# A hybrid encoder layer: DeltaNet's gate projection as filling of the chunks, and another order of the last merge

## The reference

```
h = rmsnorm(x);  parts = split(h @ w_in)                       # nq, nk, nv, nz, nba belong to DeltaNet
y_gdn = rmsnorm(o_f + o_b, norm_g) * silu(nz)                  # o_f, o_b: chunked delta rule, both ways
merged = sum_i sigmoid(h @ merge_w[i] + merge_b[i]) * (y_i @ branch_up[i])      # i = 3 is DeltaNet
x = x + merged @ mix_out
x = x + cross_attention(rmsnorm(x), rmsnorm(mem))
x = x + moe(rmsnorm(x));  return rmsnorm(x)                    # 32 experts, two per token
```

## Time and profile before

| | us |
|---|---|
| Median of three executions | 2064.29 |
| The profiled execution, its own time | 2065.67 |
| Its span in the profile | 2063.9 |
| TensorE busy | 1909.5 (93%) |
| VectorE busy | 1388.5 (67%) |
| ScalarE busy | 1083.7 (53%) |
| TensorE in the chain that ended last | 79% of the span |

### The profile page before, as it was taken

How to read it: one execution, slowest core, us unless ns; L and a number is a source line. 1 busy time by engine, 2 the same in 40 slices (tenths; PEclk the granted TensorE clock), 3 DMA queues, 4 the chain that set the end, 5 groups by cost and what they waited for, 6 DMA issues and landing times.

```text
span 2063.9 us, 33015 instructions
## 1 busy us (share of the span) xinstructions
PE 1909.5 (93%) x13076; PEld 1138.2 (55%) x13076; DVE 1388.5 (67%) x1831; ACT 1083.7 (53%) x1582; POOL 324.1 (16%) x285
## 2 busy tenths in 40 slices
PE   6999999999999999999999999895899999999991
PEld 3464565655544545767488855685355444444440
DVE  4555533799865687634643845437799999999986
ACT  4563223666656432223333534334588888888862
POOL 6000100344300523421000000000001111111102
PEclk9999999999999999999999999997899999999995
DMA  5411111212011352332321500403799999999976
GB/s 185 161 51 42 32 42 53 66 47 57 24 39 47 118 179 83 113 108 99 138 67 48 168 32 21 167 31 152 268 423 422 422 422 421 422 422 422 422 290 261
DMA packets 140522, 360.45 MB, mean 175 GB/s; under 512 B 38224, under 2 KB 91632, under 8 KB 113776
## 3 DMA queue, kind: packets, MB, share of 16 engines
q1 hardware_dynamic: 96608, 279.57, 35.7%
q10 hardware_dynamic: 34944, 46.14, 6.4%
q0 software_dynamic: 8848, 33.03, 4.1%
HBM read 307.85 MB, written 46.66 MB: 172 GB/s over the span
## 4 chain that ended last, share of the span: by engine, by line
PE 79%; DVE 9%; ACT 5%; issue 4%; DMA 1%; SPq 1%; DVEq 0%; ACTq 0%; POOL 0%; POOLq 0%
PE psum L787 40%; PE psum L1194 24%; ACT arena L1636 2%; PE psum L1183 1%; PE psum L1118 1%; PE psum L1093 1%; DVE arena L2288 1%; PE psum L917 1%; PE psum L1212 1%; PE psum L804 1%; PE psum L1053 1%; PE psum L989 1%; DMA arena<-in_w_in_dram 1%; PE psum L979 1%; PE psum L928 1%
## 5 line engine op out<-in xcount | busy, mean ns | idle before, releaser
L787 PE MATMUL psum<-arena 128*128 128x512 f16 (+2 forms) x6000 | 1016.6, 327 | 7.7 <-issue 2.8
L787 PEld LDWEIGHTS psum<-arena 128*128 128x128 f16 x6000 | 569.6, 98 | 391.5 <-issue 23.5
L1194 PE MATMUL psum<-arena 128*128 128x512 f16 x2304 | 513.5, 382 | 15.6 <-issue 12.5
L744 DVE SCALAR_TENSOR_TENSOR arena<-arena 128x2048 f16<-128x2048 f32 x192 | 437.6, 2286 | 57.9 <-ACT arena L738 57.6
L738 ACT ACTIVATE arena<-arena 128x2048 f16<-128x2048 f32 x192 | 365.5, 1908 | 69.6 <-DMA arena<-in_w_dram 42.9
L1194 PEld LDWEIGHTS psum<-arena 128*128 128x128 f16 x2304 | 224.7, 98 | 282.4 <-issue 24.7
L1944 DVE SCALAR_TENSOR_TENSOR arena<-arena 128x512 f16<-128x512 f32 (+1 forms) x185 | 124.9, 695 | 123.0 <-ACT arena L1358 122.6
L2847 POOL DMA_INDIRECT arena<-xhat,arena x32 | 67.5, 2109 | 842.1 <-PE psum L1183 446.0
L1358 ACT ACTIVATE arena<-arena 128x512 f16<-128x512 f32 (+1 forms) x212 | 127.0, 616 | 35.8 <-PE psum L787 11.4
L1379 ACT ACTIVATE arena<-psum,arena 128x512 f32<-128x512 f32 x64 | 43.8, 684 | 149.2 <-PE psum L787 149.1
L1443 ACT ACTIVATE arena<-psum 128x512 f32<-128x512 f32 (+3 forms) x51 | 29.9, 586 | 119.8 <-PE psum L787 119.8
(11 more groups left out here) (390 smaller groups left out, 2089.6 us busy)
## 6 DMA issues: line engine op xcount, KB each, us to landing
arena<-in_w_dram SPq DMA_DIRECT2D x192, 1024.0 KB, 11.9
arena<-in_merge_w_dram SPq DMA_DIRECT2D x64, 256.0 KB, 3.0
yrows<-arena ACTq DMA_DIRECT2D x32, 512.0 KB, 7.9
arena<-in_w_in_dram SPq DMA_DIRECT2D x48, 256.0 KB, 2.8
gdn_lq<-arena ACTq DMA_DIRECT2D x8, 1024.0 KB, 4.0
arena<-gdn_lq ACTq DMA_DIRECT2D x8, 1024.0 KB, 5.1
arena<-in_xattn_wkv_dram SPq DMA_DIRECT2D x32, 256.0 KB, 2.8
yrows<-arena POOLq DMA_DIRECT2D x1, 7680.0 KB, 24.3
```

What stands on the lines that cost most here:

```text
L744: nc.vector.scalar_tensor_tensor(half_of(lo, half), half_of(XLAND[m], half), WS, half_of(hi, half), ALU.mult, ALU.subtract).then_inc(w_lo[ ...
L787: mm = nc.tensor.matmul(bank[prt[0]:prt[1], c0:c1], lhs[a](k), rhs[b](k), start=(k == 0 and a + b == 0), stop=(k == nk - 1 and a == 1))
L1194: mm = nc.tensor.matmul(PS[:, bank, :], left[a][:, k, :], right[b][:, k, columns], start=k + a + b == 0, stop=(k == n - 1 and a == 1))
```

## The change

It does these things:

1. The 16 parts of `nz` are laid between the steps of the DeltaNet stages. For that 16 places are added: one more behind part 1 of `gdn_a` for tiles 0 to 5, one between parts 0 and 1 of each `gdn_c`, one behind part 6 for tiles 0 and 1. Since parts are taken in order, all parts between move up, and `nz` comes last.
2. merge30 does its four gate groups (16 parts) first, then its four sums. `fin`, `fin_gate` and `early_in` stand ahead of it, `fin_tr` behind its eleventh part.
3. The four gates of merge30 are kept in the place where the early gates go, not in SG, so their evacuation waits only for the chunks' last state.
4. `nz` is stored elsewhere (over NK), its evacuation waits for the store of the second inverse, and `early_in` waits for `done` where it waited for `g`, since the early gates come to lie over `nz`.
5. The first `merged_pair` moves to merge33.

```diff
--- before.py
+++ after.py
@@ -33,7 +33,7 @@
 NLAND = 4
 EARLY = (2, 3, 4, 5)
 LATE = (0, 3)
-PAIRS_AT = {(3, 1, 0, 2): [(0, 2)], (3, 6, 0, 1): [(1, 2)], (3, 6, 0, 3): [(2, 2)], (3, 6, 1, 1): [(3, 2)], (3, 6, 1, 3): [(4, 2)],
+PAIRS_AT = {(3, 6, 0, 0): [(0, 2)], (3, 6, 0, 1): [(1, 2)], (3, 6, 0, 3): [(2, 2)], (3, 6, 1, 1): [(3, 2)], (3, 6, 1, 3): [(4, 2)],
             (3, 7, 0, 1): [(5, 2)], (3, 7, 0, 3): [(6, 2)], (3, 7, 1, 2): [(7, 0)]}
 PSCALE = 16.0
 NE = 32
@@ -132,7 +132,9 @@
         up = kview(A["branch_up"][i])
         for q in range(4) if i != 3 else LATE:
             pairs = [[(kind, i, 2 * q + jt, half) for half in range(2)] for jt in range(2) for kind in ("gate", "up")]
-            if (i, q) != (3, 0):
+            if (i, q) == (3, 0):
+                pairs = pairs[::2] + pairs[1::2]
+            else:
                 pairs = [[pairs[2 * jt][half], pairs[2 * jt + 1][half]] for jt in range(2) for half in range(2)]
             add(f"merge{i}{q}", [(mw[:, :, q * 256:q * 256 + 256], 0, 0), (up[:, :, q * 256:q * 256 + 256], KT, 0)],
                 [kind for pair in pairs for kind in pair])
@@ -259,7 +261,7 @@
     gdn += [("gdn_a", 0, 0), None, None]
     for i in range(TT):
         mid = {6: inv(0, 2)}.get(i, [])
-        gdn += [("gdn_a", i, 1)] + {6: inv(0, 1), 7: inv(0, 4)}.get(i, []) + [None] + [("gdn_a", i + 1, 0), None] * (i + 1 < TT) + mid
+        gdn += [("gdn_a", i, 1)] + {6: inv(0, 1), 7: inv(0, 4)}.get(i, []) + [None] * (1 + (i < 6)) + [("gdn_a", i + 1, 0), None] * (i + 1 < TT) + mid
         gdn += [("gdn_a", i, 2), ("gdn_out", i)] + [("gdn_ship", 0)] * (i == 3) + [None] * (1 + (i > 0))
         gdn += {4: [("gdn_read", 0), None], 5: inv(0, 0) + [None], 6: inv(0, 3) + [None], 7: [("gdn_ship", 1)]}.get(i, [])
     for p in range(5, 10):
@@ -268,16 +270,15 @@
     for i in range(TT):
         for part in range(7):
             gdn += [("gdn_back", 1)] * ((i, part) == (3, 1))
-            gdn += [("gdn_c", i, part)] + [None] * (1 <= part < 6)
+            gdn += [("gdn_c", i, part)] + [None] * (part < 6 + (i < 2))
             if i < 3 and part in (1, 2, 4) or (i, part) == (0, 5):
                 gdn += inv(1, 3 * i + (i > 0) + (1, 2, 4, 5).index(part))
             if part == 2 and i and i + 1 < TT:
                 gdn += [("gdn_load", i + 1), ("gdn_load_inv", i + 1)]
-    dense("nq", "nk", "nv", *merge(2), *[f"early{q}" for q in (1, 2)], between=gdn)
-    dense("nz", between=[("fin", "gdn")])
-    order += [("fin_gate", "gdn"), ("early_in",)]
+    dense("nq", "nk", "nv", *merge(2), *[f"early{q}" for q in (1, 2)], "nz", between=gdn)
     again = [x for tt in range(TT) for x in (None, ("x_again", tt))]
-    dense(*merge(3), between=[None] * 4 + [("fin_tr", "gdn"), ("mem_again",)] + [None] * 16 + [("mem_stats",)] + again)
+    dense(*merge(3), between=[("fin", "gdn"), ("fin_gate", "gdn"), ("early_in",)] + [None] * 11 + [("fin_tr", "gdn"), ("mem_again",)]
+          + [None] * 12 + [("mem_stats",)] + again)
     order.append(("merged_pair", KT - 1, 1))
     late = [None] * 3 + [("norm_stats", "mem", 2)] + [None] * 2 + [("norm_rows", "mem")] + [None] * 3 + [("norm_tile", "mem", 0)]
     late += [None] * 4 + [("norm_tile", "mem", 1)]
@@ -474,7 +475,7 @@
         RAW_OF = {"nq": RAW[0], "nk": RAW[1], "nv": RAW[0]}
         NVF = f32(UN + 2056, 2, T)
         NSQ = f32(UN + 4104, 2, T)
-        NZT = f32(UN, TT, 256)
+        NZT = f32(BR + 2048, TT, 256)
         NTMP = f32(UN + 2048, TT, 256)
         assert UN + 7680 <= 52992, UN
         NBA_ = scol(128)
@@ -644,7 +645,8 @@
 
         block = ctx.enter_context(nc.Block())
         g_of = {k: n for n, k in enumerate(kind_of)}
-        gates = [n for n, k in enumerate(kind_of) if k[0] == "gate"]
+        kept = [n for n, k in enumerate(kind_of) if k[0] == "gate" and k[1] == 3 and k[2] < EARLY[0]]
+        gates = [n for n, k in enumerate(kind_of) if k[0] == "gate" and n not in kept]
         adds = [n for n, k in enumerate(kind_of) if k[0] == "up" and k[1] != 1]
         gate_no = {n: m for m, n in enumerate(gates)}
         add_no = {n: m for m, n in enumerate(adds)}
@@ -1274,7 +1276,7 @@
                             sp.dma_start(KSTACK[h % 2][to, m, :], DKT[j % 2][rows_of, h // 2, :]).then_inc(stack_in[h], 16)
                             sp.dma_start(QSTACK[h % 2][to, m, :], DQT[j // 2][rows_of, h // 2, :]).then_inc(stack_in[h], 16)
                 elif step[0] == "early_in":
-                    sp.wait_ge(*counter("vec_fin").at("g", "gdn"))
+                    sp.wait_ge(*counter("vec_fin").at("done", "gdn"))
                     for s in range(2):
                         sp.wait_ge(gate_out[s], 16 * len(early) // 2)
                     for m, n in enumerate(early):
@@ -1366,7 +1368,12 @@
                     e = counter("act_evac")
                     if name not in ("mix", "wo"):
                         act.wait_ge(*pe_mm.at(n))
-                    if name == "gate":
+                    if n in kept:
+                        if n == kept[0]:
+                            act.wait_ge(*counter("vec_gdn").at("state", TT - 1, 1))
+                        S.activation(early_gate(kind), bank, ACT.Tanh, scale=0.5 / WS,
+                                     bias=half_b[:, 8 * kind[1] + kind[2]:8 * kind[1] + kind[2] + 1]).then_inc(*e.mark(n))
+                    elif name == "gate":
                         slot = gate_no[n] % 2
                         if gate_no[n] >= 2 and gates[gate_no[n] - 2] in early:
                             act.wait_ge(gate_out[slot], 16 * sum(m < n and gate_no[m] % 2 == slot for m in early))
@@ -1438,8 +1445,7 @@
                             elif name == "nv":
                                 act.wait_ge(*counter("vec_gdnp").at("conv", "nq", 1))
                             elif name == "nz":
-                                act.wait_ge(*counter("pe_gdn").at("o", TT - 1, 1))
-                                act.wait_ge(*counter("vec_gdn").at("state", TT - 1, 1))
+                                act.wait_ge(inv_out[1], 32)
                         S.activation(dst, src, ACT.Copy, scale=1 / WS).then_inc(*e.mark(n))
                 elif what == "x2_tile":
                     tt = step[1]
@@ -1954,9 +1960,8 @@
                     if name == "up":
                         first = kind[1] == 1
                         dst = merged[:, kind[2], kind[3] * 512:kind[3] * 512 + 512]
-                        gate = SG[gate_no[gate_of(n)] % 2]
+                        gate = early_gate(kind) if gate_of(n) in early + kept else SG[gate_no[gate_of(n)] % 2]
                         if gate_of(n) in early:
-                            gate = early_gate(kind)
                             dve.wait_ge(gate_in, 16 * len(early))
                         else:
                             dve.wait_ge(*counter("act_evac").at(gate_of(n)))
```

## The result

The changed kernel took 2079.81 us in the median of four executions (2076.60 to 2081.02), the kernel before 2063.86 (2063.22 to 2067.67) beside them. The ratio is 1.0065, 95% interval 1.0042 to 1.0087: slower by 9 to 18 us. The profiled execution is the fastest of the four, 2076.60 with a span of 2074.8, 10.9 over the span before. I had forecast +6.9 and 2071.2: the sign held, the size did not (the medians lie 16 apart), and the time lies outside the range.

The account below looks back on a forecast made before the run. TensorE was taken to bound the kernel (79% of the span), so only its waits could change. Lost 16.3 us minus gained 9.4 gave net +6.9, hence 2071.2 us; range 2063 to 2077.

Parts of the forecast that it names:

- The blockade: Behind the chunks, TensorE's third gate waits through ScalarE for late3's late load: 14.2 us lost, 2.1 more by the clock.
- the small load: First load of late3's weights, queued behind eight early gates: lands 6.3 us after issue.
- L1033: Chunk-stage waits of TensorE for a VectorE copy, filled by nz parts: 4.4 us gained, bounds 4.0 and 4.4.
- L889: TensorE's wait for the last multiply of the normalising, covered by 11 parts: 1.1 us gained.
- L1014 behind GpSimd: Chunk-stage wait behind POOL, whose load of the inverses would be issued earlier: 1.1 us gained, bounds 0 and 1.1.
- L1047: Chunk-stage wait for ScalarE's late copy, falling once instead of twice: 1.1 us gained, bounds 0 and 2.3.
- L1014 behind VectorE: Chunk-stage wait of 1.9 us, no part put there for tiles 4 to 7: stays, 0 gained.
- `nz` evacuations and conversions for merge30 ... 0, bounds 0 and 2 lost: Four evacuations and five conversions among the chunks fit ScalarE's idle time: 0 us, bounds 0 and 2 lost.
- L996: TensorE's 3.1 us wait for VectorE before the chunks: stays; the bound is that it goes, with 1.7 of clock.
- Rival C: Crowding on ScalarE opens more waits, leaving only the filling's sure gains: +12.4 us, 2076.7; chance 0.15.
- The 1.7 for the half clock at 897: Chunk-stage clock drop behind short waits vanishes with a dense part in between: 1.7 us gained, bounds 0 and 1.7.
- T: The end of the last chunk product on TensorE, 954.70 in the kernel before; the forecast counts later times from it.

Follow-up runs that it names:

- unblock: The changed kernel with early_in nine parts later, behind late3's weight loads in SyncE's queue: ratio 0.9982 to the kernel before.
- rows_first: The changed kernel with the last three rows of the second inverse ahead of the part with nz's first conversion in tile 2: ratio 1.0015 to the kernel before.
- reorder_only: The kernel before with merge30's reorder but no filling, nz staying behind the chunks and early_in waiting for done: ratio 1.0037 to the kernel before.
- after_again: The changed kernel run once more with nothing edited: ratio 1.0061 to the kernel before.

## Why the prediction was wrong

- **The blockade, 14.2 + 2.1: right.** 13.1 + 1.4 measured, and 16 us by unblock. The order of SyncE and ScalarE told it; the small load landed in 5.4, not 6.3.
- **L1033, L889, L1014 behind GpSimd: right** (4.4, 1.1, 1.1 gone). L1047: 1.4 gained for 1.1. L1014 behind VectorE: 0.5 gained for 0.
- **The step that failed is "`nz` evacuations and conversions for merge30 ... 0, bounds 0 and 2 lost".** I priced crowding on ScalarE only, and only for the conversions at the end of the chunks. The other conversions of the chunk stage had moved as well, and at tile 2 one of `nz`'s weights came ahead of three inverse rows on VectorE that `vn` needs. It cost 5.3 + 2.3 = 7.6, over three times the bound. rows_first, which changes this order alone, took it back.
- **L996 "stays": right** (3.1, now 3.5). Whether half clock follows it changes from one execution to the next, up to 2.8 us, where I had put 1.7 as if fixed. It was missing in the changed kernel's profile.
- **Rival C had the right size** (2076.7) with the right kind of cause, more waits from crowding; its waits were ScalarE's, the real one was VectorE's. It deserved more than 0.15, and its price should have been open upwards.
- **The 1.7 for the half clock at 897: not a gain that can be counted on.** It did not come again, but neither did it in reorder_only, which has the steps of the kernel before and all its waits there but one of 0.3 us. The waits of 0.3 to 0.4 at tile 6 of the kernel before (915.93, 917.69) had no drop behind them either. I went by one row and took a drop that comes and goes for a fixed cost. I had gone by the row against the rule of the Trainium skill (TensorE: Matmul & The Clock Gate, section What's actually happening) that activity releases the half rate; by that rule the drop would have stayed. It did not stay, but no run here tells what had set it off.
- **The sum with measured terms:** 6.9 + 6.3 (stages up to T) - 1.8 (behind T) = 11.4, against 11.3 in the traces at L1095. Some of it is luck. Up to T the changed kernel's profile was spared the half clock behind L996 (1.7) and at 897 (1.7), both in the profile before. Without that the stages up to T would have lost 1.4 where they gained 2.0. The two drops further on that only the kernel before had are another 3.0. Such differences are the size of the 5 us by which the medians lie further apart than the profiles; how much of the 5 they make is not shown.

## What to carry to other kernels

Parts used as filling carry more than their matmuls: whatever the planner counts by parts moves with them. Go through every engine's order for the whole stage, and at each latency-bound step ask what now stands ahead of it that waits for a third engine. A weight conversion whose load is queued behind a wait on late data blocks each engine that converts, so issue the load first. A cover counts only if the chain under it doesn't wait for the cover's own end. And a drop of the clock seen in one profile is no fixed price: look for the same wait in a second profile before counting it.

## What the runs showed of the hardware

- Half clock is not certain after a wait of 3.5 us: of the nine profiles of the changed kernel and its variants that have that wait at L998, five had some 3 to 7 us at 0.5 behind it and four had none. It is not ruled out by shorter ones: behind the 2.0 us at L1118 (in the variants mostly L1120) it came in six of the 13 profiles, behind the 2.7 at L1132 (L1134) in seven. Behind the nine waits of 4.2 to 13.5 us in and behind the chunks it came each time.
- Executions of one kernel differ in step with the granted clock. Of the 24 of the kernel before beside the first experiments the fastest (2049.29) had 0.978, the slowest (2065.28) 0.969.
- VectorE's operations with two SBUF inputs took up to 4.9 times as long beside GpSimd (0.93 against 0.19 us for 128x30, 1.08 against 0.24 for 128x84), while GpSimd's pairs took 2.50 and 2.03 us in the changed kernel and the same in rows_first, where no row of the inverse ran beside them.
- A load of 256 KB behind eight others on the same queue landed in 5.4 us in the changed kernel and in 5.8 in after_again, against 3.0 on a quiet one.
